# Loading the first modulation third by columns, two rows at a time, in a four-layer transformer kernel

## The reference, cut to what matters

```python
c_act = jax.nn.silu(c)
cc_act = jax.nn.silu(c_ctx)
...
    mod = (c_act @ w_mod[l] + b_mod[l])[:, None, :]
    modc = cc_act @ w_mod[l] + b_mod[l]
    sh1, sc1, g1, sh2, sc2, g2 = jnp.split(mod, 6, axis=-1)
    ...
    px = (rmsnorm(x, norm1_g[l]) * (1.0 + sc1) + sh1) @ w_in[l] + b_in[l]
    pc = (rmsnorm(xc, norm1_g[l]) * (1.0 + scc1) + shc1) @ w_in[l] + b_in[l]
```

## Time and profile before

| | us |
|---|---|
| median of 3 runs (2296.63 to 2302.48) | 2301.42 |
| the profiled execution | 2298.28 |
| its span, first to last instruction | 2296.8 |
| PE busy in it | 2180.9 (95%) |
| DVE busy | 1100.8 (48%) |
| ACT busy | 854.8 (37%) |

### The profile page before, as it was taken

One profiled execution on the slowest core, in us unless ns is written; L12 is line 12 of the kernel. 1 busy time (PEld: TensorE's weight loads), 2 busy tenths in 40 slices (PEclk: granted clock), 3 DMA queues, 4 the chain that ended last, 5 costly groups with the idle time before them and its releaser, 6 DMA issues.

```text
span 2296.8 us, 28576 instructions
## 1 busy us (share of the span) xinstructions
PE 2180.9 (95%) x11924; PEld 1673.4 (73%) x11924; DVE 1100.8 (48%) x1938; ACT 854.8 (37%) x1320; POOL 62.4 (3%) x72
## 2 busy tenths in 40 slices
PE   6999789999999898799999999999999999998999
PEld 3766577777776776799976447777777777647999
DVE  5383844223223665755564433423332455556555
ACT  3434234222222554454554333322122344355443
POOL 1000010000000000000000001000000100000000
PEclk9999799999999999899999999999999999999999
DMA  9563023554446424456544002445444322203564
GB/s 347 185 220 110 1 74 131 172 161 161 165 124 223 155 86 149 145 161 207 149 145 168 16 1 74 152 151 160 142 147 131 108 91 74 74 1 102 171 210 124
DMA packets 263216, 308.09 MB, mean 134 GB/s; under 512 B 5424, under 2 KB 250416, under 8 KB 250800
## 3 DMA queue, kind: packets, MB, share of 16 engines
q1 hardware_dynamic: 258384, 301.62, 40.3%
q10 hardware_dynamic: 4704, 4.65, 0.6%
HBM read 305.21 MB, written 1.05 MB: 133 GB/s over the span
## 4 chain that ended last, share of the span: by engine, by line
PE 84%; DVE 9%; ACT 4%; issue 2%; DMA 1%; ACTq 0%; SPq 0%; DVEq 0%
PE bank L455 83%; DVE weights_low L1107 2%; DVE scratch L1099 1%; DMA modulation_slots<-w_mod 1%; DVE yT L1099 1%; ACT weights_high L1796 1%; DVE big L1099 1%; PE bank L464 1%; DVE input_low L1099 1%; DVE big L1634 0%; ACT L1786 0%; DVE big L1517 0%; DMA parameter_columns<-p_columns 0%; ACT rstd L1843 0%; DVE big L1206 0%
## 5 line engine op out<-in xcount | busy, mean ns | idle before, releaser
L455 PE MATMUL bank<-input_high,weights_high 128*128 128x512 f32 (+1 forms) x2336 | 821.8, 352 | 22.3 <-DVE input_low L1099 13.2
L455 PE MATMUL bank<-input_low,weights_high 128*128 128x512 f32 (+1 forms) x2336 | 807.2, 346 | 0.0
L455 PE MATMUL bank<-input_high,weights_low 128*128 128x512 f32 (+1 forms) x2336 | 806.5, 345 | 0.0
L1107 DVE TENSOR_TENSOR weights_low<-weight_slots,weights_high 128x1024 fp32r<-128x1024 f32 (+2 forms) x420 | 462.7, 1142 | 407.6 <-ACT weights_high L1796 406.6
L455 PEld LDWEIGHTS bank<-input_high,weights_high 128*128 128x128 f32 x2336 | 441.0, 189 | 137.5 <-issue 49.8
L455 PEld LDWEIGHTS bank<-input_high,weights_low 128*128 128x128 f32 x2336 | 440.8, 189 | 60.6
L455 PEld LDWEIGHTS bank<-input_low,weights_high 128*128 128x128 f32 x2336 | 441.1, 189 | 56.9 <-issue 1.0
L1796 ACT ACTIVATE weights_high<-weight_slots 128x1024 fp32r<-128x1024 f32 (+2 forms) x420 | 386.2, 967 | 176.3 <-PE bank L455 163.6
L455 PE MATMUL bank<-hidden_high,weights_high 128*128 128x256 f32 (+1 forms) x704 | 239.9, 341 | 0.6 <-DVE weights_low L1107 0.4
L455 PE MATMUL bank<-hidden_low,weights_high 128*128 128x256 f32 (+1 forms) x704 | 237.3, 337 | 0.0
L455 PE MATMUL bank<-hidden_high,weights_low 128*128 128x256 f32 (+1 forms) x704 | 237.2, 337 | 0.0
(11 more groups left out here) (241 smaller groups left out, 1596.9 us busy)
## 6 DMA issues: line engine op xcount, KB each, us to landing
modulation_slots<-w_mod SPq DMA_DIRECT2D x48, 1024.0 KB, 5.1
modulation_slots<-mod_w SPq DMA_DIRECT2D x48, 1024.0 KB, 5.0
weight_slots<-w_gu SPq DMA_DIRECT2D x44, 1024.0 KB, 5.1
weight_slots<-ffn_w_in SPq DMA_DIRECT2D x44, 1024.0 KB, 5.1
weight_slots<-w_in SPq DMA_DIRECT2D x24, 1024.0 KB, 5.4
weight_slots<-w_down SPq DMA_DIRECT2D x16, 768.0 KB, 4.9
weight_slots<-ffn_w_out SPq DMA_DIRECT2D x16, 768.0 KB, 4.8
weight_slots<-od_w_in SPq DMA_DIRECT2D x12, 1024.0 KB, 5.1
```

The source lines that it names most:

```text
L455: return pe.matmul(o, w, r, start=start, stop=stop, skip_group_check=shared)
L1107: tt(m.w_low[:, g % 2, c], m.ring[:, g % SLOTS, c], m.w_high[:, g % 2, c].bitcast(F32), ALU.subtract).then_inc(m.low_made.sem, 1)
```

## The change

The first third is cut the other way. A piece is 256 columns of all 1024 rows of `w_mod[0]` (1 MB as before, now 1 KB in a stretch and not 8 KB): piece 2i holds the shifts of rows 2i and 2i + 1, piece 2i + 1 their scales. After each two pieces a pair of rows is complete: ACT copies the bank (`pair_out`), PE turns it and sums four partial sums (`first_turn`, with a matrix `summed` that DVE makes once by a `tensor_reduce` of the identity), DVE adds the bias and makes the gains of two rows (`first_pair`). Pieces 2 to 7 and turns 1 to 3 stand inside the first projection tiles (`loading`), whose order is now row by row for both items. `keep_busy` and the one `bias(0)`, `gains(0, 0)` at the start are gone. Item 1 is loaded right behind item 0, ahead of pieces 2 to 7, and item 2 takes its old place ahead of the tables.

```diff
+FIRST_LOADED = tuple((j, k) for k in range(KD - 2) for j in range(2)) + ((0, KD - 2), (0, KD - 1), (1, KD - 2), (1, KD - 1))
+PAIRS_OF_ROWS = KD // 2
...
-                before = g + 6 if g >= 0 else 2
+                before = g + 6 if g >= 0 else 3
...
+    def pair_rows(self, i):
+        return self.scr[:, i % 2 * TOK:(i % 2 + 1) * TOK]
...
+        if third == 0:
+            at = D * (s % 2) + 256 * (s // 2)
+            sp.dma_start(m.side[:, s % SIDES, :].rearrange("p (k c) -> p k c", k=KD),
+                         w[:, at:at + 256].rearrange("(k p) c -> p k c", p=P)).then_inc(m.side_filled[s % SIDES], 16)
+            return
...
     weights(0)
+    weights(1)
     for s in range(SIDES, KD):
         step(s)
-    weights(1)
+    weights(2)
...
-    for g in range(2, len(m.item)):
+    for g in range(3, len(m.item)):
...
+    def first_piece(s):
+        i, what = divmod(s, 2)
+        pe.wait_ge(m.side_filled[s % SIDES], 16 * (s // SIDES + 1))
+        if s == 0:
+            pe.wait_ge(*m.conditions.at(0, 1))
+        elif what == 0 and i >= 2:
+            pe.wait_ge(*m.biased.at(0, i - 2))
+        for k in range(KD):
+            j = k % 4
+            o = mm(bank[4 + i % 2][32 * j:32 * j + 32, 256 * what:256 * what + 256], m.cvec[:, k, :],
+                   m.side[:, s % SIDES, 256 * k:256 * k + 256], k < 4, k >= 4)
+        o.then_inc(m.stepped.sem, 1)
+    def first_turn(i):
+        pe.wait_ge(*m.mod_out.at(0, i))
+        for c in range(4):
+            o = mm(bank[4 + i % 2][:, 2 * c:2 * c + 2], m.pair_rows(i)[:, c * P:(c + 1) * P], m.summed[:, :], True, True)
+        o.then_inc(m.mod_turned.sem, 1)
...
+    def loading(k):
+        if k < KD - 2:
+            first_piece(k + 2)
+            if k % 2:
+                first_turn(k // 2 + 1)
+    def first_tiles(items, n, place, ready, first=False):
+        for j, k in FIRST_LOADED if first else FIRST:
+            if first and j == 0:
+                loading(k)
...
-        if L == 0:
-            pe.wait_ge(*m.tables_in.end(0))
         for e in range(4, 8):
             projected_tile(L, e, n)
         pe.wait_ge(*m.gate_w_set.end(L))
+        if L == 0:
+            pe.wait_ge(*m.tables_in.end(0))
...
-    pe.wait_ge(*m.consts.end(0))
-    for k in range(KD):
-        mod_step(k)
-        if k in (4, 6):
-            add_squares(("first", k // 2 - 2), (X, C)[k // 2 - 2], m.first_squared)
-    pe.wait_ge(*m.columns_in.end(0))
-    mod_turn(0)
-    keep_busy(6, 8)
+    pe.wait_ge(*m.consts.at(0, 7))
+    for s in range(SIDES):
+        first_piece(s)
+    for half, t in enumerate((X, C)):
+        add_squares(("first", half), t, m.first_squared)
+    pe.wait_ge(*m.columns_in.end(0))
+    pe.wait_ge(*m.consts.end(0))
+    first_turn(0)
...
+    def first_pair(i):
+        r = slice(2 * i, 2 * i + 2)
+        dve.wait_ge(*m.mod_turned.at(0, i))
...
+        tt(o, bank[4 + i % 2][:, 0:8].rearrange("p (s k v) -> p s k v", s=2, k=2), b, ALU.add).then_inc(m.biased.sem, 1)
+        dve.wait_ge(*m.biased.at(0, i))
+        for v in range(2):
+            muladd(m.coef[:, 0, v, r], m.mods[:, 0, v, 8 + 2 * i:10 + 2 * i], 1.0, column(L_TAB[0], N1 + 2 * i, 2), ALU.add,
+                   ALU.mult).then_inc(m.gains.sem, 1)
...
             if k >= 2:
                 dve.wait_ge(*m.norm_low.at(part, i - 2 * per))
+            if L == 0 and which == 0 and i % (2 * per) == 0:
+                first_pair(k // 2)
+                dve.wait_ge(*m.gains.at(0, k + 1))
             muladd(m.t_[:, k % 2, t], xT[:, k, t], m.coef[:, which, v, k:k + 1], rs[:, t], ALU.mult, ALU.mult).then_inc(m.norm_t.sem, 1)
             if i >= per:
                 low(i - per)
...
     low_weights(0)
     dve.wait_ge(*m.columns_in.end(0))
-    bias(0)
-    gains(0, 0)
+    dve.tensor_reduce(m.summed[:, :], m.ident[:, :].rearrange("p (j r) -> p r j", j=4)[:, 0:2, :], AX.X, ALU.add).then_inc(m.consts.sem, 1)
...
+    def pair_out(i):
+        act.wait_ge(*m.stepped.at(0, 2 * i + 1))
+        if i >= 2:
+            act.wait_ge(*m.mod_turned.at(0, i - 2))
+        F(m.pair_rows(i), bank[4 + i % 2][:, :], ACT.Copy).then_inc(m.mod_out.sem, 1)
...
+            if L == 0 and which == 0 and i % (2 * per) == 0:
+                pair_out(k // 2)
             act.wait_ge(*m.norm_t.at(part, i))
```

More of the change, by code:

```diff
@@ L306, in signals @@
         self.tile_done = S("weight_tile_multiplied", (0, self.item[-1].last_tile + 1))
-        self.consts, self.conditions = S("constants_set", (0, 8)), S("conditions_activated", (0, 4))
+        self.consts, self.conditions = S("constants_set", (0, 9)), S("conditions_activated", (0, 4))
         self.params_v, self.lam_exp = S("parameters_derived", (0, 9)), S("lambda_exponents", (0, 2))
[L311 to L314, removed]
+        n = 11 + PAIRS_OF_ROWS
+        self.stepped, self.mod_out, self.mod_turned = S("modulation_steps_multiplied", (0, 96)), S("modulation_rows_out", (0, n)), S(
+            "modulation_turned", (0, n))
+        self.biased, self.gains = S("modulation_biased", (0, n)), S(
+            "norm_gains_made", (0, 2 + 2 * PAIRS_OF_ROWS), (1, 4), (2, 5), (3, 4))
         halves = [("first", half) for half in range(2)]
@@ L481, in mod_turn @@
         picked = ident[:, :].rearrange("p (j r) -> p j r", j=4)[:, :, 0:2]
-        rows = m.mod_rows(third)
-        pe.wait_ge(*m.mod_out.at(0, third))
+        pe.wait_ge(*m.mod_out.at(0, m.third_at(third)))
         for c in range(4):
-            i = mm(m.mod_bank(third)[:, 8 * c:8 * c + 8].rearrange("p (j v) -> p j v", j=4), rows[:, c * P:(c + 1) * P], picked, True, True)
+            i = mm(m.mod_bank(third)[:, 8 * c:8 * c + 8].rearrange("p (j v) -> p j v", j=4), m.rs[:, c * P:(c + 1) * P], picked, True, True)
         i.then_inc(m.mod_turned.sem, 1)
+    def first_piece(s):
[15 more added lines that the diff above has]
+        o.then_inc(m.mod_turned.sem, 1)
     def modulate(*place):
@@ L507, in keep_busy @@
             mm(bank[b][:, 0:P], m.mean_d[:, :], ident[:, :], True, True)
-    def first_tiles(items, n, place, ready):
-        for j, k in FIRST:
+    def loading(k):
[7 more added lines that the diff above has]
+                loading(k)
             if k in (0, KD // 2):
@@ L902, in even_mixer @@
         pe.wait_ge(*m.even_set.end(0))
-        pe.wait_ge(*m.mod_out.at(0, 8))
+        pe.wait_ge(*m.mod_out.at(0, m.third_at(8)))
         even_turn(0)
@@ L1128, in modulate @@
             bias(m.mod_turn[place])
+    def first_pair(i):
+        r = slice(2 * i, 2 * i + 2)
+        dve.wait_ge(*m.mod_turned.at(0, i))
+        o = m.mods[:, 0, :, 0:16].rearrange("p v (s k) -> p s k v", s=2)[:, :, r, :]
+        b = cols[:, L_TAB[0], B_MOD:B_MOD + 16].rearrange("p (s k) -> p s k", s=2)[:, :, r].unsqueeze(3).to_broadcast([P, 2, 2, 2])
+        tt(o, bank[4 + i % 2][:, 0:8].rearrange("p (s k v) -> p s k v", s=2, k=2), b, ALU.add).then_inc(m.biased.sem, 1)
[3 more added lines that the diff above has]
+                   ALU.mult).then_inc(m.gains.sem, 1)
     def gains(l4, which):
         at, s = ((N1, 8), (N2, 32))[which]
-        dve.wait_ge(*m.biased.at(l4, 2 * which))
+        dve.wait_ge(*m.biased.at(0, m.third_at(3 * l4 + 2 * which)))
         for v in range(2):
@@ L1141, in normed @@
             dve.wait_ge(*m.root.at(also, 1))
-        dve.wait_ge(*m.gains.at(L, 2 * which + (2 if L == 2 else 1)))
+        if L or which:
+            dve.wait_ge(*m.gains.at(L, 2 * which + (2 if L == 2 else 1) if L else 2 * PAIRS_OF_ROWS + 1))
         def low(i):
@@ L1437, in mixer_out @@
         n = N_OUT[L]
-        dve.wait_ge(*m.biased.at(L, 1))
+        dve.wait_ge(*m.biased.at(0, m.third_at(3 * L + 1)))
         for e in range(KD):
@@ L1810, in modulate @@
         act.wait_ge(*m.stepped.at(0, KD * third + KD - 1))
-        F(m.mod_rows(third), m.mod_bank(third)[:, :], ACT.Copy).then_inc(m.mod_out.sem, 1)
+        F(rs[:, :], m.mod_bank(third)[:, :], ACT.Copy).then_inc(m.mod_out.sem, 1)
         if third == 5:
@@ L1849, in coming_weights @@
             next_weights(m.proj[L][(e + 1) // 2])
+    def pair_out(i):
[3 more added lines that the diff above has]
+        F(m.pair_rows(i), bank[4 + i % 2][:, :], ACT.Copy).then_inc(m.mod_out.sem, 1)
     def normed(which, L, n, second, halves=range(1, 2)):
         part, per = (("mix", "ffn")[which], L), n // SEQ
-        act.wait_ge(*m.biased.at(L, 2 * which))
+        if L or which:
+            act.wait_ge(*m.biased.at(0, m.third_at(3 * L + 2 * which)))
         for i in range(KD * per):
@@ L2237, in scalar_program @@
     high_weights(0)
-    modulate("start", KD - 1)
     for L in range(2):
```

11 lines of the change are left out of this document (6 added, 5 removed).

## The result

The changed kernel takes 2329.68 us (4 runs, 2327.8 to 2331.11) against 2300.24 for the kernel before: 1.29% more, ratio 1.0129, 95% interval 1.0111 to 1.0147. The forecast was 2315, range 2304 to 2322. It is slower, as forecast, but by 29.4 us and not by 15. The profiled execution has a span of 2326.3 us, 29.5 over before.

A forecast was written before the change was run, and what follows sets the result against it. The prediction took PE, busy 95% of the span, as the bound, with gains only where it waits. Terms -9.8 + 23.3 + 0.8 = +14.3 us gave 2312.6, with the runs' median 3.1 higher 2315.7, stated as 2315, range 2304 to 2322.

The forecast's parts named there:

- the mechanism and the sign: First tiles start sooner but take longer, with PE idle around each turn; slower by 14.3 us, chance of slower 0.76.
- The loads of the pieces: Pieces 4 to 7 land 4.9 us after issue, with over 10 us between uses, so their loads stay hidden.
- from there the same stretches as before, 14 later: After the first tiles end near 81 us, everything runs as before, only 14 us later.
- A: The start: the first projection matmul comes at 34.4 us instead of 44.2, 9.8 us back.
- B: The first tiles' duration: 47.1 us against 23.8, 23.3 us lost, through pieces, turns, idle PE and clock falls.
- wait for item 2 and the rest behind them: Behind the first tiles: item 0 ends only 2.8 us ahead of item 1, covering less of item 2's making; 0.8 lost.
- two falls: In the first tiles, the granted clock falls after two of three turns, 2.3 us each, 4.6 us in B.
- unchanged: Rival on the start: queues do not share by packets, ctx stays at 22.43; sum +20.7 us, chance 0.10.
- earlier still: Rival on the start: ACT's queue has the engines alone, first matmul at 27.9; +3.2 us, up to +10; chance 0.14.
- the turns are covered: Rival in the first tiles: row k's tiles do not wait behind first_pair, the clock holds; sum +0.2 us, chance 0.16.

The follow-up runs named there:

- lows_first: The changed kernel with DVE making the low parts of the row before a pair ahead of first_pair, not behind it: 2313.25 us, ratio 1.0062.
- experiments 1 and 2: First, the changed kernel with sum_of_parts allocated last: 2317.58 us; second, the kernel before with an unused 8-byte tensor in the change's place: 2309.58 us.
- the repeats: The kernel before and the changed kernel, both unchanged, profiled once more: 2298.99 us and 2326.57 us.
- filled: The changed kernel with two 512-column matmuls, read by nobody, behind each of turns 1 to 3: 2320.13 us, ratio 1.0095.
- turn_between: lows_first with the turn moved on PE between the two items' tiles of the odd row: 2313.44 us, ratio 1.0061.
- before_moved_with_weights: The kernel before with an unused 64-byte tensor ahead of weights_high, so weights and arena move together: 2300.09 us, ratio 1.0001.
- placed_lows: The changed kernel with sum_of_parts allocated last and the lows of the row before made ahead of first_pair: 2302.40 us, ratio 1.0013.

## Why the prediction was wrong

**Right, the mechanism and the sign.** The first tiles start sooner and take much longer; idle of 0.72 (0.75 forecast) ahead of each turn and of 2.31 (2.4) behind it, the second released by DVE's `input_low`; a piece takes 1.07 (1.06), a turn 1.05 (0.95); the order of DVE's program is the reason, which `lows_first` shows by taking the three waits away. The loads of the pieces were hidden: the slots' loads never show as a wait of PE behind piece 1.

**The step that failed: "from there the same stretches as before, 14 later".** It took for granted that what the diff doesn't touch keeps its pace. The allocation of 8 bytes moved the arena by 64, and the matmuls of 256 columns in layers 1 and 3 start every 120.0 and not every 116.7 ns: 10.5 of the 29.5 us. Shown from both sides (experiments 1 and 2: -9.0 and +11.4 us of span). No term of the sum had it, and none of the rivals. `after_placed`, the same change with that tensor elsewhere, takes 2317.58 us, inside the forecast's range.

**Terms that were mis-sized**, 4.7 us together against a sum of 14.3 (19.0 measured at the marker):

| term | forecast | measured | 
|---|---|---|
| A, the first matmul sooner by | 9.8 | 6.3 |
| B, the first tiles longer by | 23.3 | 24.8 |
| wait for item 2 and the rest behind them | 0.8 | 0.5 |

(B: from 37.89 to about 86.5, the start of the last matmul, 86.22, and its 0.23, is 48.6; less 23.8.) The column is for the pair of profiles that the forecast used. Against the repeats A is 8.0, since before started later there, and the lag 16.1; that the changed kernel starts at 37.9 and not at 34.4 holds in both.

A: `ctx` was in at 19.76 and not at 16.0. The shares were right: from 7 to 12 us the queues moved, in the changed kernel,

```profile
q10 hardware_dynamic: 855, 0.87, 55.5%
q1 hardware_dynamic: 862, 0.87, 54.0%
```

equal packets and equal bytes. But from 4.5 to 6.5 us ACT's queue had nearly none, though `x` was issued at 1.22 and the queue's condition columns were through:

```profile
q1 hardware_dynamic: 707, 0.71, 102.8%
q10 hardware_dynamic: 46, 0.04, 6.9%
```

I had the condition columns through at 3.3 us and `x` right behind them; their last packet is of 4.6, and `x` ran from about 6, with an equal share from 7. It was in at 13.72 and not at 10.0, and `ctx` behind it is late by the same 3.7. From `ctx` on the forecast holds: 18.1 us to the first projection matmul, 18.4 forecast.

B: the clock fell behind all three turns, not two: 0.50 at 46.4, 63.5 and 77.2. The forecast took 4.6 us for two falls, `filled` puts all three at 5.3. By the rule of the Trainium skill ("TensorE: Matmul & The Clock Gate", section "HAM oscillation — how this bites in real kernels"), bursts shorter than the wait between them start at the low clock every time. Here the turn is such a burst, 1.05 us ahead of a wait of 2.31, and the trace agrees in so far as all three fell. But only the first of the three rows began at the low clock; the other two began at full pace, at 62.71 and 76.40, and the clock fell 0.8 us later:

```profile
62.71 0.50 PE L472 MATMUL bank<-input_high,weights_high 128*128 128x512 f32 x1 [2.31 <-DVE input_low L1144]
63.52 0.61 PE L472 MATMUL bank<-input_high,weights_high 128*128 128x512 f32 x1
```

**The rivals.** The start was neither unchanged nor earlier still, but in between. That the turns are covered was wrong for this order. `lows_first` comes near it, with DVE's order alone: no wait behind a turn, the clock up. `turn_between` shows that the wait for the copy is not had for a move on PE: the chain of bias, gains and rows then shows.

**What stays open.** What in the addresses costs the 3.3 ns; the step from 517 to 512 in layer 1 that `after_placed` and `before_moved_with_weights` have and `placed_lows` has not; and why `x` began so late.

## What to carry to other kernels

Before you time an edit that allocates anything, allocate it behind the large tensors, or compare the pace of a stretch that the edit doesn't touch: a count of matmuls in a full window tells a layout effect (here 10 us of 29) from the edit's own. Profile both kernels twice, so that you know what repeats. When a stage is split so that pieces arrive inside the work, write down for each engine what stands in its queue *behind* the new wait: here finished inputs were held up by a wait that had nothing to do with them, which cost 7 us, and 5 more in clock. A chain that was hidden under a load wait once is not hidden when it is cut in four: each turn brings its latency again.

## What the runs showed of the hardware

- With PE full and at full clock, matmuls of 256 columns started every 116.7 or every 120.0 ns in the same code, depending on where tensors lay in SBUF: 502 or 503 in 60 us in layer 1 in the kernels with the arena moved against the weights, 512 to 517 in the others profiled here. At 512 columns a move of the arena by 64 bytes cost nothing, one by 128 bytes 0.9 ns for each matmul (234.3 against 233.4).
- While both had work, the two queues moved equal numbers of packets, in either mix of sizes: 155 and 155 packets for 1.11 and 0.13 MB, 862 and 855 for 0.87 and 0.87 MB.
- Two wide matmuls in a wait of 2.3 us kept the granted clock at 1.00. Three times, they saved 5.3 us, where the waits themselves were 7.0.
